# Gates and ups of a feed-forward stage as one 512-column product and one 256-column product, their halves added by VectorE

## The reference

```python
def conv_ffn(xn, w_gate, conv_w, conv_b, w_up, w_down):
    S = xn.shape[1]
    g = xn @ w_gate                                   # 1024 -> 2816
    gp = jnp.pad(g, ((0, 0), (CONV_WIDTH - 1, 0), (0, 0)))
    gc = conv_b + sum(conv_w[j] * gp[:, j:j + S] for j in range(CONV_WIDTH))
    h = jax.nn.gelu(gc, approximate=False) * (xn @ w_up)
    return h @ w_down                                 # 2816 -> 1024

h = h + conv_ffn(rms_norm(h, norm_ffn[i]), ...)
```

## Time and profile before

| | us |
|---|---|
| median of three runs | 1074.93 |
| the profiled execution | 1075.35 |
| its span, first to last instruction | 1072.7 |
| TensorE busy | 1064.1 |
| VectorE busy | 721.6 |
| ScalarE busy | 574.9 |

### The profile page before, as it was taken

One profiled execution on the slowest core, in us unless ns is written; L12 is line 12 of the kernel. 1 busy time (PEld: TensorE's weight loads), 2 busy tenths in 40 slices (PEclk: granted clock), 3 DMA queues, 4 the chain that ended last, 5 costly groups with the idle time before them and its releaser, 6 DMA issues.

```text
span 1072.7 us, 19921 instructions
## 1 busy us (share of the span) xinstructions
PE 1064.1 (99%) x8092; PEld 949.9 (89%) x8092; DVE 721.6 (67%) x1230; ACT 574.9 (54%) x977; POOL 141.2 (13%) x166
## 2 busy tenths in 40 slices
PE   9999999999999999999999999999999999999998
PEld 7887878656898999799999999999998799999997
DVE  5665566387554878778875676666677776766674
ACT  4532676544444567866565554444574555545454
POOL 0000010253200001632531000000023410000000
PEclk9999999999999999999999999999999999999999
DMA  9732121286613442057444364555543334555641
GB/s 382 319 137 66 75 79 40 93 289 213 232 41 119 141 145 80 6 193 236 148 168 158 119 236 161 194 186 170 198 155 103 134 119 153 202 201 177 211 178 39
DMA packets 25386, 168.77 MB, mean 157 GB/s; under 512 B 3280, under 2 KB 3536, under 8 KB 5456
## 3 DMA queue, kind: packets, MB, share of 16 engines
q1 hardware_dynamic: 25152, 167.25, 44.1%
q10 hardware_dynamic: 144, 0.26, 0.1%
HBM read 164.35 MB, written 1.05 MB: 154 GB/s over the span
## 4 chain that ended last, share of the span: by engine, by line
PE 96%; DVE 2%; ACT 2%; issue 0%; DVEq 0%; ACTq 0%
PE bank L437 26%; PE bank L438 25%; PE bank L439 25%; PE bank L1550 2%; PE bank L494 2%; PE bank L1714 2%; PE bank L1704 2%; PE bank L1694 1%; PE bank L1577 1%; PE bank L1568 1%; PE bank L446 1%; PE bank L2363 1%; PE bank L1395 1%; DVE wlo L415 1%; ACT TILE L1753 1%; PE bank L1688 1%
## 5 line engine op out<-in xcount | busy, mean ns | idle before, releaser
L437 PE MATMUL bank<-OPH,whi 128*128 128x256 f32 (+1 forms) x1716 | 519.7, 303 | 0.3
L439 PE MATMUL bank<-OPH,wlo 128*128 128x256 f32 (+1 forms) x1716 | 511.2, 298 | 0.0
L438 PE MATMUL bank<-OPL,whi 128*128 128x256 f32 (+1 forms) x1716 | 511.2, 298 | 0.0
L415 DVE TENSOR_TENSOR wlo<-raw,whi 128x1024 fp32r<-128x1024 f32 (+1 forms) x255 | 304.0, 1234 | 101.4 <-ACT whi L400 101.3
L437 PEld LDWEIGHTS bank<-OPH,whi 128*128 128x128 f32 x1716 | 328.0, 191 | 17.3 <-issue 5.2
L438 PEld LDWEIGHTS bank<-OPL,whi 128*128 128x128 f32 x1716 | 328.2, 191 | 10.0 <-issue 1.2
L439 PEld LDWEIGHTS bank<-OPH,wlo 128*128 128x128 f32 x1716 | 328.0, 191 | 9.8
L400 ACT ACTIVATE whi<-raw 128x1024 fp32r<-128x1024 f32 (+1 forms) x255 | 254.9, 1050 | 74.2 <-PE bank L439 71.9
L437 PE MATMUL bank<-whi,OPH 128*128 128x256 f32 (+2 forms) x272 | 93.8, 345 | 0.2 <-DVE OPL L717 0.2
L438 PE MATMUL bank<-wlo,OPH 128*128 128x256 f32 (+2 forms) x272 | 91.1, 335 | 0.0
L439 PE MATMUL bank<-whi,OPL 128*128 128x256 f32 (+2 forms) x272 | 91.1, 335 | 0.0
(11 more groups left out here) (291 smaller groups left out, 1132.6 us busy)
## 6 DMA issues: line engine op xcount, KB each, us to landing
raw<-in_stream SPq DMA_DIRECT2D x143, 1024.0 KB, 4.9
PROJ<-in_stream SPq DMA_DIRECT2D x5, 1024.0 KB, 18.4
raw<-in_stream SPq DMA_DIRECT2D x4, 1056.0 KB, 8.6
PROJ<-PROJ SPq DMA_DIRECT2D x32, 64.0 KB, 3.9
FIRST<-in_first SPq DMA_DIRECT2D x1, 1248.0 KB, 5.9
C<-in_con SPq DMA_DIRECT2D x1, 1157.5 KB, 7.2
FIRST<-in_first SPq DMA_DIRECT2D x1, 1024.0 KB, 8.0
WST<-in_w_s SPq DMA_DIRECT2D x2, 256.0 KB, 7.3
```

What stands on the lines that cost most here:

```text
L415: nc.vector.tensor_tensor(c.w[1][:, part], c.raw[:, part], c.w[0][:, part].bitcast(F32), ALU.subtract).then_inc(*raises(c.lo[h]))
L437: nc.tensor.matmul(out, w[0], x[0], start=start, stop=False, skip_group_check=skip)
L438: nc.tensor.matmul(out, w[0], x[1], start=False, stop=False, skip_group_check=skip)
L439: return nc.tensor.matmul(out, w[1], x[0], start=False, stop=stop, skip_group_check=skip)
```

## The change

- OPH and OPL become the two halves of one tensor OPS, `[P, KD, 2, T]`, so that a block's high and low parts can be read as one moving operand of two runs of 256 columns.
- A new function `products_apart` replaces `products` for gates and ups: one matmul of 512 columns, high weights by high and low activations, into a whole bank, high x high in columns 0 to 255 and high x low in 256 to 511; and one of 256 columns, low weights by high activations, added to the first half. The two halves are not summed on TensorE.
- Each of the two blocks t of 128 features has a bank of its own. A gate takes banks 2 and 3, an up banks 0 and 1, in every step.
- ScalarE copies the second halves of both banks to `part` (`copy_halves`), VectorE adds them to the first halves (`add_halves`), which empties the banks; the multiplication by r then works in place on the sum, in SBUF.
- In step 0 the gate's copy stands before the split of up 1's weights and the root on ScalarE, and its add before the low half of that split on VectorE. The copy of an up stands behind the Gelu.
- At the end of feed-forward 0 the second half of the last split moves behind the operand's first two blocks on both engines, and the load of the table for logarithm and exponential behind the last blocks that this stage gives. Some semaphore names change.

```diff
-        OPH, OPL = sb("OPH", [P, KD, T], F32R), sb("OPL", [P, KD, T], F32R)
+        OPS = sb("OPS", [P, KD, 2, T], F32R)
+        OPH, OPL = OPS[:, :, 0, :], OPS[:, :, 1, :]
...
+        def products_apart(bank, w, k, lo, start, stop):
+
+            both = bank[:].rearrange("p (a b) -> p a b", b=SEQ)
+            nc.tensor.matmul(both, w[0], OPS[:, k, :, lo:lo + SEQ], start=start, stop=False, skip_group_check=True)
+            return nc.tensor.matmul(bank[:, 0:SEQ], w[1], OPH[:, k, lo:lo + SEQ], start=False, stop=stop,
+                                    skip_group_check=True)
...
+            g_both, up_both = twin[1], twin[0]
+            part = {what: PROJ[:, at:at + 512].rearrange("p (a b) -> p a b", b=SEQ)
+                    for what, at in (("gate", 9224), ("up", 9736))}
             for c in range(NF):
-                g.append(GBANK.take("pe", ("dve",)))
-                up.append(GBANK.take("pe", ("dve",)))
+                g.append([b.take("pe", ("dve",)) for b in banks[2:4]])
+                up.append([b.take("pe", ("dve",)) for b in banks[0:2]])
...
-            def wide(e, u, ch):
-                for point in due(e, u.empty, ch.lo):
-                    e.wait_ge(*point)
-                for t in range(2):
+            def wide(e, us, ch):
+                for point in due(e, ch.lo):
+                    e.wait_ge(*point)
+                for t, u in enumerate(us):
+                    for point in due(e, u.empty):
+                        e.wait_ge(*point)
                     for k in range(KD):
-                        for point in due(e, op_block(k)):
-                            e.wait_ge(*point)
-                        mm = products(u.mem[:, t * SEQ:(t + 1) * SEQ], cols(ch, k, t * P, P), op(k, lo, SEQ), k == 0,
-                                      k == KD - 1)
-                mm.then_inc(*raises(u.full))
+                        mm = products_apart(u.mem, cols(ch, k, t * P, P), k, lo, k == 0, k == KD - 1)
+                    mm.then_inc(*raises(u.full))
+
+            def copy_halves(e, what, c, us, both):
+                for point in due(e, us[0].full, us[1].full, ("halves_summed", l, c - 1, what) if c else None):
+                    e.wait_ge(*point)
+                nc.scalar.activation(part[what], both[:, :, SEQ:2 * SEQ], ACT.Copy).then_inc(
+                    *raises(("low_copied", l, c, what)))
+
+            def add_halves(e, what, c, out, both):
+                for point in due(e, ("low_copied", l, c, what)):
+                    e.wait_ge(*point)
+                nc.vector.tensor_tensor(out, both[:, :, 0:SEQ], part[what], ALU.add).then_inc(
+                    *raises(("halves_summed", l, c, what)))
...
                 for k in range(KD):
-                    for u, ch in both:
-                        for point in due(e, u.empty, ch.lo[k // 4], op_block(k)):
+                    for us, ch in both:
+                        for point in due(e, [u.empty for u in us], ch.lo[k // 4], op_block(k)):
                             e.wait_ge(*point)
...
                 log_exp_table()
+                copy_halves(e, "gate", 0, g[0], g_both)
                 split_hi(e, first.s + 4)
                 inverse_root(e, f"ffn{l}", r, total.tot.mem[:, 0:SEQ], 1.0 / D, total.full, total.tot.read["act"])
                 for c in range(NF):
                     j = 2 * c
                     split_hi(e, by["gate", c].s + (3 if c else 4))
+                    if c:
+                        copy_halves(e, "gate", c, g[c], g_both)
...
                     nc.scalar.activation(t1[c].mem[:], t1[c].mem[:], ACT.Gelu).then_inc(*raises(("gelu_made", l, c)))
+                    copy_halves(e, "up", c, up[c], up_both)
...
-                log_exp_table()
-                split_hi(e, by["down", NF - 1].s + 3)
+                if l:
+                    log_exp_table()
+                split_hi(e, by["down", NF - 1].s + 2.5)
                 for i in range(1, 4 if l == 0 else 1):
                     s.gives.act(e, (2 * i - 2, 2 * i - 1))
+                    if i == 1:
+                        split_hi(e, by["down", NF - 1].s + 3)
+                log_exp_table()
...
-                    nc.vector.tensor_tensor(pad[c % 2][:, :, 2:SEQ + 2], two(g[c].mem), rr, ALU.mult).then_inc(*raises(("gate_scaled", l, c)))
+                    add_halves(e, "gate", c, padded, g_both)
+                    if c == 0:
+                        split_lo(e, first.s + 4)
+                    for point in due(e, ("halves_summed", l, c, "gate"), ("factor_made", f"ffn{l}")):
+                        e.wait_ge(*point)
+                    nc.vector.tensor_tensor(padded, padded, rr, ALU.mult).then_inc(*raises(("gate_scaled", l, c)))
...
-                    nc.vector.tensor_tensor(two(t2[c].mem), two(up[c].mem), rr, ALU.mult).then_inc(*raises(up[c].read["dve"]))
-                    for point in due(e, ("gelu_made", l, c), up[c].read["dve"]):
+                    add_halves(e, "up", c, two(t2[c].mem), up_both)
+                    for point in due(e, ("halves_summed", l, c, "up")):
+                        e.wait_ge(*point)
+                    nc.vector.tensor_tensor(two(t2[c].mem), two(t2[c].mem), rr, ALU.mult).then_inc(*tick("dve"))
...
-                split_lo(e, by["down", NF - 1].s + 3)
+                split_lo(e, by["down", NF - 1].s + 2.5)
                 for i, a in enumerate(acc if l == 0 else ()):
...
                     if i:
                         s.gives.dve(e, (2 * i - 2, 2 * i - 1))
+                    if i == 1:
+                        split_lo(e, by["down", NF - 1].s + 3)
...
             for c in range(NF):
-                g[c].freed[:] = [("gate_scaled", l, c)]
+                for i in range(2):
+                    g[c][i].freed[:] = [("halves_summed", l, c, "gate")]
+                    up[c][i].freed[:] = [("halves_summed", l, c, "up")]
```

More of the change, by code:

```diff
@@ L2896, in pe @@
                 for k in range(KD):
-                    for u, ch in both:
-                        for point in due(e, u.empty, ch.lo[k // 4], op_block(k)):
+                    for us, ch in both:
+                        for point in due(e, [u.empty for u in us], ch.lo[k // 4], op_block(k)):
                             e.wait_ge(*point)
-                        for t in range(2):
-                            mm = products(u.mem[:, t * SEQ:(t + 1) * SEQ], cols(ch, k, t * P, P), op(k, lo, SEQ),
-                                          k == 0 and t == 0, k == KD - 1, skip=True)
-                        if k == KD - 1:
-                            mm.then_inc(*raises(u.full))
+                        for t, u in enumerate(us):
+                            mm = products_apart(u.mem, cols(ch, k, t * P, P), k, lo, k == 0, k == KD - 1)
+                            if k == KD - 1:
+                                mm.then_inc(*raises(u.full))
                 total.add(e)
@@ L2952, in dve @@
                     j = 2 * c
-                    split_lo(e, by["gate", c].s + (3 if c else 4))
-                    for point in due(e, g[c].full, ("factor_made", f"ffn{l}"), ("pads_zeroed", l, c % 2)):
+                    padded = pad[c % 2][:, :, 2:SEQ + 2]
+                    if c:
+                        split_lo(e, by["gate", c].s + 3)
+                    for point in due(e, ("pads_zeroed", l, c % 2)):
                         e.wait_ge(*point)
@@ L2968, in dve @@
                             if tap:
[L2969 removed]
+                                ins.then_inc(*raises(("conv_done", l, c, "older", b)))
                             else:
[L2971 removed]
+                                ins.then_inc(*raises(("conv_done", l, c) if b else ("conv_done", l, c, "half")))
                         if tap:
[L2973 removed]
+                            e.wait_ge(*when(("conv_done", l, c, "older", 1)))
                     split_lo(e, by["up", c].s + 3)
[L2975 removed]
+                    for point in due(e, t2[c].empty):
                         e.wait_ge(*point)
[L2977 to L2978 removed]
+                    add_halves(e, "up", c, two(t2[c].mem), up_both)
+                    for point in due(e, ("halves_summed", l, c, "up")):
+                        e.wait_ge(*point)
+                    nc.vector.tensor_tensor(two(t2[c].mem), two(t2[c].mem), rr, ALU.mult).then_inc(*tick("dve"))
+                    e.wait_ge(*ticked("dve"))
+                    for point in due(e, ("gelu_made", l, c)):
                         e.wait_ge(*point)
@@ L3005, in ffn @@
             s.used = [("down_added", l, NF - 1)]
-            s.operand_used = [up[NF - 1].full]
+            s.operand_used = [up[NF - 1][1].full]
             return s
```

8 lines of the change are left out of this document (2 added, 6 removed).

## The result

The changed kernel takes 1084.32 us (median of 4 runs, 1084.02 to 1084.72) against 1074.93 for the kernel before beside it: ratio 1.0088, 95% interval 1.0071 to 1.0106. It is slower by 9.4 us; 1074.1 was forecast, and the upper end of the range was 1079.5. The profiled execution took 1084.4 us with a span of 1082.6, 9.9 above the 1072.7 of before.

A forecast was written before the change was run, and what follows sets the result against it. TensorE was taken as the bound. Layer 0 -0.10, its end +0.40 and layer 1 -1.10 sum to -0.8 us, the 9.5 saved spent almost whole on the two starts: 1074.1 us forecast, range 1071.5 to 1079.5.

The forecast's parts named there:

- Bound and method: Whole kernel: TensorE busy 1064.1 of 1072.7 us; matmul time saved comes off the end, waits ahead of TensorE are added.
- Start of layer 0, gate 1: First feed-forward's start: gate 1 waits 0.7 us for gate 0's copy and add, starting at 12.35 after the stage's first product.
- The split of up 1's weights ... stands behind the copy: 11.41, +0.35: Layer 0's start, ScalarE: up 1's weight split moves from 11.06 to 11.41 us; root, scaling, taps and Gelu shift as much.
- The rest of that sum: Layer 0's start after gate 1: up 1 waits 2.62 us, gate 2 0.90, up 2 0.68; gate 3 starts 3.36 later.
- the rows chosen: Durations taken from profile rows of 512 elements: 0.60 us per ScalarE copy, 0.69 per VectorE add.
- What the products give: Gates and ups: a 512- plus a 256-column matmul take 0.3465 us instead of 0.360, saving 9.5 us in two layers.
- The bounds: Wide product between 0.213 us (columns alone, saves 9 us more) and 0.240 (twice the 256-column one, saves nothing).
- Steady state: From gate 3 on: VectorE keeps 1.6 and 1.3 us free per period, so copies and adds are hidden.
- End of layer 0: Latent products: the moved half split makes block 2 ready at 20.25, due at 19.94, costing +0.40 us; table load hidden.
- a rival given 0.07: TensorE's clock falls in the starts' new waits: one fall costs 2.7 us, two 5.3, giving 1079.4; chance 0.07.
- The product costing as much as two: Gates and ups: the 512-column product takes as long as two 256-column ones, nothing saved: 1082.5 us; chance 0.06.

The follow-up runs named there:

- three narrow products: The early split with the 512-column product made as two of 256 columns, same weights, into the two halves of the bank: 1084.74 us.
- the wait added: Kernel before, with ScalarE waiting for gate 0's product ahead of splitting gate 1's and up 1's weights, both layers: 1081.43 us, ratio 1.0061.
- the old end: The early split with the end of layer 0 (last latent split and table load) put back as in the kernel before: 1080.89 us.
- the grouped order: The early split with eight high 512-column products, then eight low 256-column ones, in gates and ups behind the first two: 1076.50 us, ratio 1.0021.
- the early split: Changed kernel with gate 1's weights split ahead of the copy of gate 0 on ScalarE, both layers: 1079.19 us, ratio 1.0045.

## Why the prediction was wrong

Step by step, by its own parts:

- *Bound and method.* TensorE is the bound, and what the starts lose comes off the end: right. The waits and gains at gate 3 stood in the span.
- *Start of layer 0, gate 1.* This is the step that failed. Its line "The split of up 1's weights ... stands behind the copy: 11.41, +0.35" moves only up 1's split, and the description of the change says the same. The edit puts the copy, and with it the wait for gate 0, ahead of one call that splits gate 1's weights too, and in the kernel before this half of the call had run at 589.51, beside the joint block. The prediction had gate 1 wait for the add alone (0.7); the weights hold it to 15.77. Undoing that line brings 5.1 us of the 10.2 by which the forecast missed. I had asked what queues behind the copy, and taken the answer from the one instruction that stood there before, not from all that the call issues.
- *The rest of that sum* holds once the line is undone: waits of 0.85 and 2.5 ahead of gate 1 and up 1 where 0.7 and 2.62 were summed, gate 3 at 50.33. That this meets the forecast to the hundredth is luck: down 0 starts 0.28 late (26.43 for 26.15), and gate 2 is held 0.3 less than summed. The copies took 0.594 and the adds 0.69, both at the rows chosen.
- *What the products give.* 0.3465 a pair, by two rows of runs of one width. The pair does take that in the joint blocks and in a few more products, but 0.353 in all from gate 3 on. That is the mis-sized term: 4.6 us in place of 9.5; from the gate 3s on it is 3.0 in place of 6.9, and 3.9 us of the miss. The bounds held it.
- *Steady state.* VectorE hides copies and adds: right, TensorE meets no new wait from gate 3 to up 10.
- *End of layer 0.* +1.10 in place of +0.40. The sum took VectorE's half split at 1.23 with 0.1 of waiting for ScalarE where it waits 0.92, and it did not have VectorE come later out of its last chunk.
- *Rivals.* The clock did fall, by a rival given 0.07, though behind gate 1's wait and not up 1's, and it cost nothing: its price was worked out as if TensorE had nothing to wait for behind it. The product costing as much as two was half true. None of the rivals was the missed queue.

Against the Trainium skill's rule ("TensorE: Matmul & The Clock Gate", section "Back-to-back issue gap", N/2.4 + 2.5 ns, which the section gives for the isolated gap of a single matmul) the prediction went by its rows. By that rule the pair would be 0.325 and the merging worth 1.8 us, as an estimate. The traces go with the rows: the three narrow products take 0.360, the pair 0.3467 or 0.3533, and the merging is worth 4.6.

## What to carry to other kernels

When an instruction that waits is put ahead of a call, list every instruction that the call issues, find when each of them ran before, and look for those that ran early: it is they that pay, not the ones already waiting. A wait on an engine at half load costs the full amount if it stands ahead of the operands for the engine that is the bound. And before a striking change of the clock is blamed, see whether the next product could have started sooner: here the clock's price was nothing where another wait stood behind it, and 1 to 2 us where none did.

## What the hardware showed that I had not expected

- Products of 512 and 256 columns in alternation have two paces: 0.3467 us a pair, which is the sum of 0.2265 and 0.120 of the runs of one width, or 0.3533. Each product of 16 pairs keeps one, and one trace holds both, at the same clock and with no wait between. In groups of eight they take 0.230 and 0.119. Whether the 512 columns are one run or two makes no difference. What decides the pace these runs do not tell.
- TensorE's clock fell to 1.2 GHz behind the waits of 3.7 us idle in the changed kernel, in both layers, for 6.8 us. Behind waits of 2.2 to 2.6 us it fell in some places of the profiled executions and not in others: in both layers with three narrow products, in layer 0 alone in the kernel before with the wait added and in the one with the old end, in layer 1 alone with the grouped order, in neither with the early split alone. It differs between executions of one kernel too: with the grouped order six have a mean clock of 1.000 and take 1075.98 to 1076.53 us, four have 0.996 to 0.998 and take 1077.63 to 1078.36. So where nothing hides it, the fall cost some 2 us there. What decides whether it falls these runs do not tell.
- 34 products of ones, 128 columns in float32, took 7.5 us, each showing as two matmuls of 0.11 us.
